# Four borders between stages of a two-layer HGRN2/Mamba2 kernel: one low weight part made early, the scaled y in PSUM, and matmuls into an unread bank in TensorE's pauses

## The reference

```
h  = rmsnorm(x, pre_norm) * (1 + scale) + shift          # scale, shift, gate: from c @ ada_w + ada_b
y  = mixer(h)   or   (silu(conv(h @ w_up[:, :F])) * (h @ w_up[:, F:])) @ w_down
x  = x + gate * rmsnorm(y, post_norm)
```

## Time and profile before

| | |
|---|---|
| median of three executions | 1371.37 us (1370.68 to 1371.9) |
| the profiled execution, its own time | 1371.69 us |
| its span (first to last instruction) | 1370.0 us |
| mean granted TensorE clock | 0.992 |
| DVE (VectorE), ACT (ScalarE), POOL (GpSimd) busy | 880.2, 657.1, 338.7 us |
| DMA | 183.21 MB, mean 134 GB/s |

### The profile page before, as it was taken

The page is one execution under the profiler, slowest core; times in us unless marked ns, Lnnn a source line. Parts: engine busy times, 40 slices in busy tenths (PEclk is TensorE's granted clock), DMA queues, the critical chain, the costliest instruction groups (busy, mean ns, idle before and its releaser), DMA issues.

```text
span 1370.0 us, 21017 instructions
## 1 busy us (share of the span) xinstructions
PE 1304.0 (95%) x7893; PEld 1100.9 (80%) x7893; DVE 880.2 (64%) x1718; ACT 657.1 (48%) x1037; POOL 338.7 (25%) x236
## 2 busy tenths in 40 slices
PE   5999999999997999999999989999999989899997
PEld 2678888888774888888888857888888869799997
DVE  4577776677778544322444787777777876875673
ACT  4445444444345433323333256455555644764664
POOL 1000000000202655305552020111111230683771
PEclk9999999999999999999999999999999999999999
DMA  9644333336461532234323432633333348376753
GB/s 345 189 132 130 123 124 123 107 94 215 154 200 46 166 103 84 70 102 122 101 86 123 112 123 79 183 93 93 93 93 93 95 156 242 98 203 170 219 156 108
DMA packets 274790, 183.21 MB, mean 134 GB/s; under 512 B 6642, under 2 KB 249106, under 8 KB 274706
## 3 DMA queue, kind: packets, MB, share of 16 engines
q1 hardware_dynamic: 274162, 180.00, 43.7%
q10 hardware_dynamic: 544, 2.10, 0.4%
HBM read 181.03 MB, written 1.05 MB: 133 GB/s over the span
## 4 chain that ended last, share of the span: by engine, by line
PE 77%; DVE 12%; ACT 5%; DMA 2%; issue 2%; SPq 1%; POOL 1%; DVEq 0%; ACTq 0%
PE bank L2175 18%; PE bank L2177 18%; PE bank L2176 18%; DVE wl L1373 3%; ACT wh L841 2%; DMA gates<-in_ada_w 1%; PE bank L2200 1%; PE bank L2201 1%; PE bank L2202 1%; PE bank L2251 1%; PE bank L2187 1%; PE bank L2185 1%; PE bank L2186 1%; DMA wraw<-in_mb_w_out 1%; PE bank L2806 1%
## 5 line engine op out<-in xcount | busy, mean ns | idle before, releaser
L2175 PE MATMUL bank<-hh,wh 128*128 128x512 f32 (+1 forms) x1298 | 456.4, 352 | 7.8 <-DVE wl L1373 3.6
L2177 PE MATMUL bank<-hh,wl 128*128 128x512 f32 (+1 forms) x1298 | 451.8, 348 | 0.0
L2176 PE MATMUL bank<-hl,wh 128*128 128x512 f32 (+1 forms) x1298 | 451.3, 348 | 0.0
L841 ACT ACTIVATE wh<-wraw 128x1024 fp32r<-128x1024 f32 (+2 forms) x265 | 256.8, 985 | 72.8 <-PE bank L2177 50.7
L2175 PEld LDWEIGHTS bank<-hh,wh 128*128 128x128 f32 x1298 | 244.0, 188 | 42.8 <-DVE wl L1373 6.1
L1373 DVE TENSOR_TENSOR wl<-wraw,wh 128x1024 fp32r<-128x1024 f32 (+2 forms) x171 | 188.6, 1124 | 138.1 <-ACT wh L841 138.1
L1830 DVE SCALAR_TENSOR_TENSOR conv<-bank,pv,conv 128x189 f32<-128x189 f32 (+3 forms) x396 | 172.5, 436 | 153.2 <-ACT conv L1112 138.3
L2177 PEld LDWEIGHTS bank<-hh,wl 128*128 128x128 f32 x1298 | 244.0, 188 | 32.5
L2176 PEld LDWEIGHTS bank<-hl,wh 128*128 128x128 f32 x1298 | 244.1, 188 | 30.3
L729 POOL TENSOR_TENSOR wl<-wraw,wh 128x1024 fp32r<-128x1024 f32 (+2 forms) x87 | 199.2, 2295 | 197.2 <-ACT wh L841 196.8
L775 POOL TENSOR_TENSOR hl<-yT,hh 128x512 fp32r<-128x512 f32 x13 | 18.9, 1481 | 369.1 <-DVE gates L1730 356.5
(11 more groups left out here) (346 smaller groups left out, 2087.8 us busy)
## 6 DMA issues: line engine op xcount, KB each, us to landing
wraw<-in_ffn_w_up SPq DMA_DIRECT2D x88, 512.0 KB, 4.0
araw<-in_ada_w SPq DMA_DIRECT2D x40, 1024.0 KB, 7.4
wraw<-in_mb_w_in SPq DMA_DIRECT2D x48, 512.0 KB, 4.0
wraw<-in_hg_w_in SPq DMA_DIRECT2D x40, 512.0 KB, 3.8
wraw<-in_ffn_w_down SPq DMA_DIRECT2D x32, 512.0 KB, 4.0
wraw<-in_mb_w_out SPq DMA_DIRECT2D x16, 512.0 KB, 4.7
gates<-in_ada_w SPq DMA_DIRECT2D x5, 1024.0 KB, 9.4
wraw<-in_hg_w_out SPq DMA_DIRECT2D x8, 512.0 KB, 5.0
```

Source lines behind the costliest of these rows:

```text
L841: act.activation(slot(whp, n, 0, size), wraw[:, n % SLOTS, 0:size], ACT.Copy).then_inc(w_hi, 1)
L2175: pe.matmul(dst, W, hi(k), start=(k == 0), stop=False, **skip)
L2176: pe.matmul(dst, W, lo(k), start=False, stop=False, **skip)
L2177: ins = pe.matmul(dst, L, hi(k), start=False, stop=(k == nk - 1), **skip)
```

## The change

Seven edits. (1) In `variance` VectorE now makes one low weight part before it waits for rstd; ScalarE makes its high part ahead of `rsqrt`. (2) The scaled y is written to bank 6 of PSUM instead of the SBUF buffer sq. At 256 columns its two tiles fit side by side (`at6`) and it is made one tile ahead as before, but for tile 1, which is now made after L1500 of tile 0; at 512 columns there is room for one tile, and the next is scaled only after L1500 has read xT. (3) As bank 6 held the ada_w product, ScalarE copies that to asum ahead of `second_rsqrt`, and VectorE waits for the copy. (4) The other low part (borders two and four) comes after tile 1 instead of tile 0. (5) TensorE waits for the fourth weight tile's low part only before that tile's first matmul. (6) `stay_busy`: 18, 18, 9 and 16 matmuls of 512 columns into a bank that nobody reads and that the next group starts anew, at the end of TensorE's work before each pause. (7) The constant BUSY.

```diff
+BUSY = (18, 18, 9, 16)
 # ScalarE, border 1 (2 and 4 in the same way)
+        split_hi(at["up", 0, 0, 1, 1])
         rsqrt(("ss", 0, 0), T, D, square=2, hold=("r", 0, 0))
-        split_hi(at["up", 0, 0, 1, 1])
+        ada_rows(LATE + 3)
         second_rsqrt(0, T)
         shift_high(0, 0, 1)
-        ada_rows(LATE + 3)
         ada_rows(LATE + 4)
 # ScalarE, border 4
+        split_hi(at["m", KT - 1, 0] + SLOTS)
         rsqrt(("ss", 1, 0), SEQ, D, square=6, hold=("r", 1, 0))
-        for j in range(2):
-            split_hi(at["m", KT - 1, j] + SLOTS)
+        split_hi(at["m", KT - 1, 1] + SLOTS)
+        ada_rows(LATE + 11)
         second_rsqrt(2, SEQ)
         shift_high(2, 1, 1, SEQ)
-        ada_rows(LATE + 11)
 # VectorE
-        def variance(l, s, n):
+        def variance(l, s, n, early):
+            split_lo(early)
             u, w = sq[:, 0, 0:n], sq[:, 1, 0:n]
...
-        def add_and_norm(l, s, n, weights):
+        def add_and_norm(l, s, n, rows, weight=None):
...
             def turn(m):
-                ins = V.tensor_tensor(sq[:, m % 2, 0:n], yT[:, m, 0:n], bank[plan.bank(first)][:, 0:n], ALU.mult)
+                ins = V.tensor_tensor(bank[6][:, at6(m):at6(m) + n], yT[:, m, 0:n], bank[plan.bank(first)][:, 0:n], ALU.mult)
...
+            at6 = lambda m: m % 2 * SEQ if n == SEQ else 0
             dve.wait_ge(rb_ready, i + 1)
+            plan.wait_emptied(dve, ("am", rows))
             turn(0)
...
-                    ins = V.scalar_tensor_tensor(out=xT[:, m, r], in0=sq[:, m % 2, r], scalar=gsc[:, l, s, m, b:b + 1],
+                    ins = V.scalar_tensor_tensor(out=xT[:, m, r], in0=bank[6][:, at6(m) + r.start:at6(m) + r.stop], scalar=gsc[:, l, s, m, b:b + 1],
                                                  in1=xT[:, m, r], op0=ALU.mult, op1=ALU.add)
...
-                if m < KT - 1:
+                if n == SEQ and 1 <= m < KT - 1:
                     turn(m + 1)
...
-                if m == 0:
-                    for w in weights:
-                        split_lo(w)
+                if m < KT - 1 and (m == 0 or n == T):
+                    turn(m + 1)
+                if m == 1 and weight is not None:
+                    split_lo(weight)
...
-        variance(0, 0, T)
-        add_and_norm(0, 0, T, (u0 + 3,))
+        variance(0, 0, T, u0 + 3)
+        add_and_norm(0, 0, T, LATE + 3)
...
-        variance(0, 1, T)
-        add_and_norm(0, 1, T, (at["b", 0] - 1, at["b", 0]))
+        variance(0, 1, T, at["b", 0] - 1)
+        add_and_norm(0, 1, T, LATE + 5, at["b", 0])
...
-        variance(1, 0, SEQ)
-        add_and_norm(1, 0, SEQ, [at["up", 1, 0, 1, j] for j in range(2)])
+        variance(1, 0, SEQ, at["up", 1, 0, 1, 0])
+        add_and_norm(1, 0, SEQ, LATE + 11, at["up", 1, 0, 1, 1])
 # TensorE, by_tile (last = the fourth tile's piece)
+                    if last is not None and k == 0 and dst is products[-1][0]:
+                        need_sub(last)
...
+        def stay_busy(b, n, piece):
+
+            pe.wait_ge(w_hi, piece + 1)
+            for _ in range(n):
+                pe.matmul(bank[b][:, :], slot(whp, piece, 0, P), slot(whp, piece, 0, T), start=True, stop=True)
...
         ada_block(LATE + 3)
         ada_block(LATE + 4)
+        plan.wait_emptied(pe, ("y", 0, 4))
+        stay_busy(0, BUSY[0], at["up", 0, 0, 0, 0])
...
                             ada_block(LATE + 5)
                             ada_block(LATE + 6)
+                            stay_busy(2, BUSY[1], at["xs", 0, 0])
...
+        plan.wait_free(pe, ("y", 1, 2))
+        stay_busy(2, BUSY[2], at["m", 0, 0])
         pe.wait_ge(yl_ready, 2 * KT)
...
         ada_block(LATE + 11)
+        plan.wait_emptied(pe, ("at", LATE + 10))
+        stay_busy(3, BUSY[3], at["up", 1, 0, 0, 0])
```

More of the change, by code:

```diff
@@ L1195, in _ @@
         psum_freed_dve = plan.freed["dve"]
+        split_hi(at["up", 0, 0, 1, 1])
         rsqrt(("ss", 0, 0), T, D, square=2, hold=("r", 0, 0))
-        split_hi(at["up", 0, 0, 1, 1])
+        ada_rows(LATE + 3)
         second_rsqrt(0, T)
         shift_high(0, 0, 1)
-        ada_rows(LATE + 3)
         ada_rows(LATE + 4)
         ffn_act(0, T, True)
+        split_hi(at["b", 0] - 1)
         rsqrt(("ss", 0, 1), T, D, square=4, hold=("r", 0, 1))
-        for j in (1, 0):
-            split_hi(at["b", 0] - j)
+        split_hi(at["b", 0])
+        ada_rows(LATE + 5)
         second_rsqrt(1, T)
         shift_high(1, 1, 0)
-        ada_rows(LATE + 5)
         ada_rows(LATE + 6)
@@ L2188, in gemm_ks, with by_tile @@
             return ins
-        def by_tile(count, products, n=T, ks=range(KT)):
+        def by_tile(count, products, n=T, ks=range(KT), last=None):
             hi, lo = act_tiles(n)
@@ L2529, in ffn_pe @@
                     need_sub(u0 + 2)
-                    need_sub(u0 + 3)
                     up = lambda u, part: (bank[2 * u + part][:, 0:n], tile_w(u0 + 2 * u + part), KT,
@@ L2534, in ffn_pe @@
                     if l == 0:
-                        by_tile(hl_count - KT, first, n)
+                        by_tile(hl_count - KT, first, n, last=u0 + 3)
                     else:
-                        by_tile(hl_count - KT, first, n, range(KT - 3))
+                        by_tile(hl_count - KT, first, n, range(KT - 3), last=u0 + 3)
                         for one in first:
@@ L2647, in _ @@
         first = (("xs", 0, 0), ("dt",), ("xs", 0, 1), ("b", 0))
-        need_sub(at[("b", 0)])
+        need_sub(at[("b", 0)] - 1)
         for key in first:
@@ L2651, in _ @@
         by_tile(2 * KT, [(bank[plan.bank(key)][0:64, :] if key == ("dt",) else dst(key), tile_w(at[key], 64 if key == ("dt",) else P), KT,
-                          lambda ins, key=key: plan.done(ins, key)) for key in first])
+                          lambda ins, key=key: plan.done(ins, key)) for key in first], last=at[("b", 0)])
         def dt_turns():
```

## The result

The changed kernel takes 1364.55 us (median of six, 1362.48 to 1365.1) where the kernel before took 1371.63 (six runs beside it): a ratio of 0.9942, 95% interval [0.9932, 0.9952] (the quotient of the two medians is 0.9948, so the gain is 7.1 us by medians and 8 us by the ratio). Two later comparisons of five executions each gave medians of 1364.87 and 1364.64, ratios 0.9945 and 0.9944. The forecast was 1364.2, faster. The profiled execution took 1364.83 us.

The account below looks back on a forecast made before the run. TensorE, busy 1304.0 of 1370.0 us, bounds the kernel, so only its pauses and low-clock work can give time. Borders 2.1 + 3.2 + 0 + 1.9 = 7.2 us give 1364.2 us against the median, range 1362.5 to 1368.5.

Parts of the forecast that it names:

- Products hold the clock: Pauses at the borders: products into an unread bank keep full clock, 1.6 us in border one, 2.5 in border two.
- Rival A: All borders: the products don't hold the clock; only 3.1 us gained, 1368.3 us; chance 0.10.
- Tile 0 earlier by 0.47: Border one: tile 1 is no longer scaled between L1487 and L1500 of tile 0, so L1500 starts 0.47 us earlier.
- rival C: Three borders: the asum copy is late, everything behind bank 6 slips up to 1.0 us each; 1367.2 us; chance 0.12.
- It fits, with 0.1 to spare: Border one: the asum copy ends at 422.9, before VectorE's first L1472 at 422.96; cost nothing, bound 1.0 us.
- 2.24 us a tile: 512 columns: dependent steps on VectorE take 2.24 us a tile without stalls, under TensorE's 2.72, so nothing after tile 0 waits.
- Border two, 3.2: Border two: TensorE starts 0.75 us earlier, first products at full clock save 2.5; together 3.1 to 3.3, taken as 3.2.
- Border three, 0: Border three: 1.5 us saved by the held clock become waiting for a low part's raw weights; bounds 0 and 1.5, taken 0.
- the loads ahead are released by VectorE, not by TensorE: Border three: weight loads queued on SP don't depend on TensorE, so its saved 1.5 us become waiting.
- a wait for DMA near 1141 of about 2 us: After border three: the sign named for the saved time turning into waiting, a longer DMA wait of about 2 us.
- Border four, 1.9: Border four, 256 columns: last L1500 1.4 us earlier, plus 0.5 for ScalarE's copy gone from there; bounds 0.7 to 2.2.
- Rival B: Borders one, two, four: L1487 still stalls behind GpSimd, 3.3 us a tile, VectorE the pacemaker; +2.7, 1374.1 us; chance 0.06.

Follow-up runs that it names:

- no products: The changed kernel with BUSY = (0, 0, 0, 0), no products into an unread bank, all else as changed: 1369.08 us, ratio 0.998 to the kernel before.
- with half: The changed kernel with 9, 9, 5 and 8 products in place of 18, 18, 9 and 16: 1367.35 us, ratio 0.9956 to the kernel before.
- none in the third: The changed kernel with BUSY = (18, 18, 0, 16), without the nine products of border three: 1365.34 us, ratio 0.9944 to the kernel before.
- The version with both pauses filled: The changed kernel plus nine products ahead of border one's sums, eight near 87 us, and border four's scaled y in bank 5: 1362.43 us, ratio 0.9927.

## Why the prediction was right, step by step

*Products hold the clock (1.6 in border one, 2.5 in border two).* Right. In the ten profiles with at least the full number in borders one, two and four, k = 0 was taken up at 1.00 in all thirty borders one, two and four; without products (before, no products) it was low in all six. Border one got 1.60 as said. Rival A falls.

*Tile 0 earlier by 0.47.* The mechanism was right, the size wrong. From the sums to L1504 it is 10.55 us where it was 10.83, thus 0.28. L1463 to L1474 takes 0.47 where L1461 to L1472 took 0.34, because VectorE waits for the asum copy, and L1491 to L1504 takes 0.98, not 0.92. That first 0.13 is rival C in small, and by the prediction's own list ("if L1472 of tile 0 waits for ScalarE") a sign against it. In border four the copy is the last to come (0.43 idle); bank 5 gave 0.28 of it back. "It fits, with 0.1 to spare" was too tight a sum to be called nothing.

*2.24 us a tile.* It is 2.31 (430.74 less 428.43), still under TensorE's 2.72; no tile is waited for in border one, and L1491 lost its stalls. Undoing the place alone brought back five of twelve, so the bank frees L1491 of GpSimd, as forecast, but most of the stalls at 512 columns went with the new order, which the prediction didn't say. The Trainium skill ("Perfetto Trace Analysis", Optimizing Scalar/DVE Operations) has the dearer access to PSUM; here L1474 to L1491 takes 0.73 us where L1472 to L1487 took 0.72, and a tile in border one takes 2.24 to 2.39 with the scaled y in SBUF where it takes 2.24 to 2.31 in PSUM, so these runs show next to nothing of it.

*Border two, 3.2.* It gave 2.7: 0.52 for the start (0.75 forecast, less for the same 0.13 and the 0.98) and 2.17. The low parts were worth what they were said to be: left late, the start alone loses 0.83.

*Border three, 0.* It came out at 0.86 in the first comparison and at 0.8 in the clean one. The step that doesn't hold is "the loads ahead are released by VectorE, not by TensorE". VectorE does release them, but waits for ScalarE's high part, and that stands in ScalarE's order behind its read of TensorE's bank. One step more back along the chain would have shown it. It costs 0.8 where the clock falls ahead of the first products, as in the run without the nine, 2.0 us after the transposes. In the kernel before, the clock fell 4.9 us after them (1122.00), and the first load left after 7.75 us as in the changed kernel, so there the step held and the 0.86 has another source. In all thirteen profiles the stretch in the table is the start of ScalarE's high part of the raw weights that are waited for near 1141 us (24.37 us after the transposes before, 23.51 changed) plus 19.9. From the first load to that start it takes 16.6 us before, 16.9 without any products and with half, and 15.7 to 16.2 in the other ten, "none in the third" among them. So the 0.86 is in the transfers and not in their release; whether the products have a part in it stays open. The sign that was named for this step, a wait for DMA near 1141 of about 2 us, did not show: the two waits there are 0.69 and 0.74, before 1.54 and 0.58. What TensorE saved became waiting elsewhere: 1.35 us at 1121.78, for VectorE's low part.

*Border four, 1.9.* It gave 1.75, within its bounds. Counted from the sums, the last L1504 comes 1.55 earlier than the last L1500 did (1.5 forecast). Behind it only 0.2 of the 0.5 for the moved copy was gained: ScalarE's next high part then waits 0.28 for TensorE's bank (1175.25).

Forecast 7.2, measured 7.15: that close only by luck: border three's 0.86 made up for 0.25, 0.5 and 0.15 that were missing elsewhere.

Rival B's price doesn't follow from its terms. Seven times 0.56 less the forecast gains (2.1 and 3.2) leaves 1.8 us in border one and 0.7 in border two, where it has 1.7 and 1.5; that would be 1373.4 and not 1374.1.

## What to carry to other kernels

Before idle work is put in to hold TensorE's clock, put in order what follows the pause: the slow products may be hiding a late tile, and alone neither half gave more than half of the whole. Fill a pause almost up to its end, for in half-filled ones the clock fell in some and held in others, while a few products too many cost little where later tiles are waited for. When a transfer's release is named, follow the releasing engine's own waits as far as they go.

## What the runs showed of the hardware

Pauses of one and the same length had different outcomes. After 2.4 us near 87 us the clock fell in 6 of the 12 profiles in which it wasn't filled, after 2.57 us ahead of the sums of border one in 4 of 11, after 4.27 us and more (ahead of k = 0, nothing filled in) in all six. Over all thirteen profiles, from 38 to 1340 us: none of the 74 pauses of more than 1.0 and up to 1.6 us was followed by the low clock, both of 1.78 and 1.92 us were, 12 of 27 from 2.2 to 2.6 us, and all nine of 2.9 us and more. The Trainium skill ("TensorE: Matmul & The Clock Gate", What's actually happening) calls the gate free-running against the kernel, and this agrees. The prediction took from three runs of the kernel before, 1.2 us apart, that what this does to the time isn't large; 26 later runs of that kernel span 3.0 us. It may make for much of the spread: of the changed kernel's 16 runs the three with a mean granted clock of 0.998 took 1362.5 to 1362.8 us, the other 13, at 0.994 to 0.997, 1364.0 to 1366.0. The version with both pauses filled spans 1.0 us in five runs; but the changed kernel's last five span only 0.5. One such fall costs 1.7 us (14.55 less 12.85 in the table's first column), so two single profiles of this kernel can't be compared by their spans to less than that; stretch by stretch they can.
